# Second attention rebuilt with tokens on partitions, its projections and output products placed inside the attention steps, and gating products opened early

## The reference

```python
g = gelu(y); val, gate = split(g @ w_glu); x = x + val * sigmoid(gate)      # gating
...
kv = rms_norm(x, kv_norm) @ kv_w                 # keys and values from x
k = rms_norm(kv[..., :1024] as (8 heads, 2, 64), k_norm); v = kv[..., 1024:] as (8 heads, 128)
q = rms_norm((rms_norm(x, attn_norm) @ w_q) as (8 heads, 2, 64), q_norm)
s = q . k * scale + relative_bias, causal        # two score maps c = 0, 1 per head
pm = softmax(s)
attn = pm[c=0] - lam * pm[c=1]                   # lam from four learned vectors
o = attn @ v                                     # 128 wide per head
o = rms_norm(o, subln) * (1 - lam_init)          # over the 128 of a head
x = x + o @ w_o
```

## Time and profile before

| | |
|---|---|
| median of 3 runs | 2135.4 us (2134.31 to 2138.55) |
| profiled execution | 2137.13 us, its span 2135.3 us |
| TensorE busy | 2039.7 us, 96% of the span |
| VectorE, ScalarE, GpSimd busy | 1230.0, 816.9, 465.5 us |
| mean granted clock of TensorE | 0.974 |
| weight loads | 308 of 512 KB |

### The profile page before, as it was taken

One profiled execution on the slowest core, in us unless ns is written; L12 is line 12 of the kernel. 1 busy time (PEld: TensorE's weight loads), 2 busy tenths in 40 slices (PEclk: granted clock), 3 DMA queues, 4 the chain that ended last, 5 costly groups with the idle time before them and its releaser, 6 DMA issues.

```text
span 2135.3 us, 26693 instructions
## 1 busy us (share of the span) xinstructions
PE 2039.7 (96%) x9714; PEld 1621.7 (76%) x9714; DVE 1230.0 (58%) x1695; ACT 816.9 (38%) x1248; POOL 465.5 (22%) x626
## 2 busy tenths in 40 slices
PE   8999999999999879999999989999888999999988
PEld 7998678888887767877878877655564877877877
DVE  5345365656355984577365557533485577365555
ACT  4323242222135874344243335322364444243333
POOL 3110039998814551000000011011100100000010
PEclk9999799999999999999999999999897999999999
DMA  4221023264442422222223232211100222223232
GB/s 144 90 80 61 20 89 109 89 217 150 167 160 81 156 84 89 89 89 92 95 98 109 75 103 99 82 62 62 50 26 20 79 89 98 90 98 109 79 99 99
DMA packets 54866, 201.69 MB, mean 94 GB/s; under 512 B 6438, under 2 KB 6950, under 8 KB 53740
## 3 DMA queue, kind: packets, MB, share of 16 engines
q1 hardware_dynamic: 47132, 166.39, 23.1%
q0 software_dynamic: 7632, 33.91, 4.4%
HBM read 184.51 MB, written 15.77 MB: 94 GB/s over the span
## 4 chain that ended last, share of the span: by engine, by line
PE 86%; DVE 9%; ACT 2%; issue 1%; DMA 1%; POOLq 0%; POOL 0%; SPq 0%; DVEq 0%; ACTq 0%
PE ps L440 69%; PE ps L612 6%; PE ps L763 2%; PE ps L572 1%; PE ps L838 1%; PE ps L554 1%; DVE t L1793 1%; PE ps L1769 1%; DVE w_lo L426 1%; DVE t L1429 1%; DVE rstd L535 0%; DVE t L564 0%; PE ps L794 0%; PE ps L1760 0%; DVE pp L1609 0%
## 5 line engine op out<-in xcount | busy, mean ns | idle before, releaser
L440 PE MATMUL ps<-x_hi,w_hi 128*128 128x512 f32 x1280 | 512.4, 400 | 2.7 <-DVE w_lo L426 2.6
L440 PE MATMUL ps<-x_lo,w_hi 128*128 128x512 f32 x1280 | 507.8, 397 | 0.0
L440 PE MATMUL ps<-x_hi,w_lo 128*128 128x512 f32 x1280 | 505.4, 395 | 0.0
L426 DVE TENSOR_TENSOR w_lo<-raw,w_hi 128x1024 fp32r<-128x1024 f32 x308 | 401.6, 1307 | 173.0 <-ACT w_hi L422 172.7
L422 ACT ACTIVATE w_hi<-raw 128x1024 fp32r<-128x1024 f32 x308 | 321.7, 1048 | 216.3 <-DMA raw<-in_wstream 143.6
L440 PE MATMUL ps<-a_hi,w_hi 128*128 128x512 f32 x864 | 345.1, 399 | 10.7 <-DVE pp L1609 4.8
L440 PE MATMUL ps<-a_lo,w_hi 128*128 128x512 f32 x864 | 342.5, 396 | 0.0
L440 PE MATMUL ps<-a_hi,w_lo 128*128 128x512 f32 x864 | 342.5, 396 | 0.0
L440 PEld LDWEIGHTS ps<-x_hi,w_hi 128*128 128x128 f32 x1280 | 241.5, 189 | 83.9 <-issue 22.9
L440 PEld LDWEIGHTS ps<-x_hi,w_lo 128*128 128x128 f32 x1280 | 241.7, 189 | 55.7
L440 PEld LDWEIGHTS ps<-x_lo,w_hi 128*128 128x128 f32 x1280 | 241.4, 189 | 55.1 <-issue 1.2
(11 more groups left out here) (364 smaller groups left out, 2544.6 us busy)
## 6 DMA issues: line engine op xcount, KB each, us to landing
raw<-in_wstream SPq DMA_DIRECT2D x308, 512.0 KB, 3.3
ev<-mix_ev POOLq DMA_DIRECT2D x8, 1024.0 KB, 5.1
mix_cp<-c_p POOLq DMA_DIRECT2D x8, 640.0 KB, 3.5
cp<-mix_cp POOLq DMA_DIRECT2D x8, 640.0 KB, 6.3
mix_ev<-v_b POOLq DMA_DIRECT2D x8, 512.0 KB, 3.5
fall<-fall POOLq DMA_DIRECT2D x4, 544.0 KB, 5.1
h<-in_xT SPq DMA_DIRECT2D x4, 528.0 KB, 7.2
mix_ev<-e_r POOLq DMA_DIRECT2D x1, 2048.0 KB, 8.5
```

The source lines that it names most:

```text
L426: e.tensor_tensor(w_lo[:, u.slot, :], raw[:, u.c % 2, :], w_hi[:, u.slot, :], ALU.subtract)\
L440: last = e.matmul(ps[:, bank, :], wt[:, u.slot, w], x[:, k0 + k, 0:SEQ], start=(k == 0 and n == 0), stop=(k == kt - 1 and n == 2))
```

## The change

The projections of the second attention are made with the tokens on partitions. The activations become the stationary side (`a_hi`, `x_hi` blocks of 128 tokens) and the weights the moving one. Six groups of 96 matmuls (`group_pe`) take the place of 24 units: query heads 0 to 3 and 4 to 7, key 0 to 3, value 0 to 3, key 4 to 7, value 4 to 7. A group has eight parts of 12 matmuls: four weight blocks c for token blocks 0 and 1, then the same four for token blocks 2 and 3. The loads follow (`load_columns`): four unit tiles by 256 columns, later two by 512. ScalarE evicts with the token's norm as scale and squares (`group_act`), VectorE sums by head and scales (`head_sums_dve`, `head_scales_dve`). Query, key and output tiles of a head are turned by TensorE (`turn_pe`) into one bank (7) and split on the way out (`turn_act`, `turn_dve`); `TURN` numbers the turns in TensorE's order, and each waits for the one before (`tr_ev`).

The first four groups run ahead of the loop (`attention2_first`), the last two and the output products of the first four heads stand inside the steps (`FILL`: step to part). A head's blocks now run from the widest to the narrowest. The scores use a ring of three banks. The weights are left without the first map's divisor, which goes into the norm: the output is made as queries by features, held (`dve_hold`), squared with its sum (`act_square`) and scaled (`dve_out`, with a root on ScalarE, `act_root`), per query and head, then turned back by the flip matrix. The output products have 12 matmuls in each part (`out2_pe`); those of heads 4 to 7 follow the loop. Both barriers, `normed`, all `head_*` helpers, the values' turn, the subtractions on GpSimd and the load of `spread2` are gone. GpSimd's load of p now waits for the last value product. The sums for the token norm run as four products with one column.

Apart from this, four gating units are opened before and behind the last mixer's output products, with six of their eight tiles; two weight splits move ahead for it.

The core of the diff (mere renamings, tiles in memory and the semaphores' list are left out):

```diff
+    def glu_open_pe(e, s):
+        u = Unit(U_GLU + s)
+        e.wait_ge(lo_ok, u.n(1))
+        e.wait_ge(unit_ev, U_GLU)
+        if s >= 2:
+            e.wait_ge(v_ev, KT)
+        for k in range(GLU_K):
+            if s == 0:
+                e.wait_ge(g_lo, k + 1)
+            product(e, u, s, a_hi, a_lo, k, KT)
+    def glu_close_pe(e, s):
+        u = Unit(U_GLU + s)
+        for k in range(GLU_K, KT):
+            if s == 0:
+                e.wait_ge(g_lo, k + 1)
+            last = product(e, u, s, a_hi, a_lo, k, KT)
+        last.then_inc(unit_mm, 1)
...
+    NORMED = {0: 0, 1: 1, 2: 2, 4: 3}
+    FILL = {}
+    for k, i in enumerate((0, 1, 2, 3, 5, 6, 7, 8)):
+        FILL[i] = ("group", 4, k)
+    for k, i in enumerate((9, 10, 12, 13, 14, 16, 17, 18)):
+        FILL[i] = ("group", 5, k)
+    for k, i in enumerate((21, 22, 23, 25, 26, 28, 30, 32)):
+        FILL[i] = ("out", k // 2, k % 2)
+    SPLIT_AT = {}
+    for i, (kind, a, b) in FILL.items():
+        if kind == "group" and b >= 4:
+            SPLIT_AT[i + 1] = U_Q + 4 * a + b
+        elif kind == "out" and b == 1:
+            SPLIT_AT[i + 1] = U_WO + 4 + a
...
+    def load_columns(e, n, first, count, lo):
+        e.wait_ge(lo_ok, n - 1)
+        w = KT * P // count
+        src = A["wstream"][first * P:(first + count) * P, lo:lo + w].rearrange("(a p) c -> p a c", p=P)
+        e.dma_start(raw[:, n % 2, :].rearrange("p (a c) -> p a c", a=count), src).then_inc(raw_in[n % 2], 16)
+    def load_tail(e):
+        for g, first in enumerate((U_Q, U_Q + 4, U_KV, U_KV + 8, U_KV + 4, U_KV + 12)):
+            for c in range(4):
+                load_columns(e, U_Q + 4 * g + c, first, 4, 256 * c)
+        for j in range(KT):
+            load_columns(e, U_WO + j, U_WO + 2 * (j % 4), 2, SEQ * (j // 4))
...
+    def group_bank(g, tb):
+        return (0 if g < 4 and tb >= 2 else 3) + tb % 2
...
+    def group_pe(e, g, half):
+        s, c = half // 4, half % 4
+        n = U_Q + 4 * g + c
+        hi, lo = (a_hi, a_lo) if g < 2 else (x_hi, x_lo)
+        if s == 0:
+            e.wait_ge(lo_ok, n + 1)
+        if c == 0:
+            if g == 0:
+                e.wait_ge(unit_ev, U_Q - 2 + 2 * s)
+            elif g == 4 and s == 1:
+                e.wait_ge(unit_ev, U_Q + 18)
+            elif g == 5:
+                e.wait_ge(unit_ev, U_Q + 20 + 2 * s)
+            else:
+                e.wait_ge(unit_ev, U_Q + 4 * g - 2 + 2 * s)
+        for k in (2 * c, 2 * c + 1):
+            if s == 0 and g in (0, 2):
+                e.wait_ge(xlo_ok, (40 if g == 0 else 48) + k + 1)
+            for tb in (2 * s, 2 * s + 1):
+                o = ps[:, group_bank(g, tb), :].rearrange("p (a c) -> p a c", a=4)
+                r = slice(tb * P, (tb + 1) * P)
+                for i, (x, w) in enumerate(((hi, w_hi), (lo, w_hi), (hi, w_lo))):
+                    last = e.matmul(o, x[:, k, r], w[:, n % 4, :].rearrange("p (a k c) -> p k a c", a=4, k=2)[:, k % 2],
+                                    start=(k == 0 and i == 0), stop=(k == KT - 1 and i == 2))
+        if s == 1:
+            last.then_inc(unit_mm, 1)
+        elif c == 3:
+            last.then_inc(pg_mm, 1)
...
+    def group_act(e, g, tb):
+        if tb < 2:
+            e.wait_ge(pg_mm, g + 1)
+        else:
+            e.wait_ge(unit_mm, U_Q + 4 * g + 4)
+        if g == 0 and tb == 0:
+            e.wait_ge(rstd_ok, STEP[6] + 1)
+        src, r = ps[:, group_bank(g, tb), :], rstd[:, tb:tb + 1]
+        ins = e.activation(group_store(g, tb), src, ACT.Copy, scale=r)
+        if g in NORMED:
+            k = 4 * NORMED[g] + tb
+            ins.then_inc(qn_c, 1)
+            ge(e, qn_s, k - 1)
+            ins = e.activation(sq[:, k % 2, 0:SEQ], src, ACT.Square, scale=r)
+        ins.then_inc(unit_ev, 1)
...
+    def head_sums_dve(e, g, tb):
+        k = 4 * NORMED[g] + tb
+        e.wait_ge(unit_ev, U_Q + 4 * g + tb + 1)
+        e.reduce_sum(state[:, 3 * NORMED[g], 8 * tb:8 * tb + 8],
+                     sq[:, k % 2, 0:SEQ].rearrange("p (g c) -> p g c", c=HD), AX_X).then_inc(qn_s, 1)
+    def head_roots_act(e, g):
+        r = 3 * NORMED[g]
+        e.wait_ge(qn_s, 4 * NORMED[g] + 4)
+        e.activation(state[:, r + 1, :], state[:, r, :], ACT.Sqrt, bias=eps6[:, 0:1], scale=1.0 / HD).then_inc(qn_rt, 1)
+    def head_scales_dve(e, g):
+        r = 3 * NORMED[g]
+        e.wait_ge(qn_rt, NORMED[g] + 1)
+        n = dve.did(e.reciprocal(state[:, r + 2, :], state[:, r + 1, :]))
+        e.wait_ge(dve_did, n)
+        for tb in range(4):
+            y = group_store(g, tb).rearrange("p (g c) -> p g c", c=HD)
+            e.tensor_tensor(y, y, state[:, r + 2, 8 * tb:8 * tb + 8].unsqueeze(2).to_broadcast([P, 8, HD]), ALU.mult)\
+                .then_inc(qn_y, 1)
...
+    def turn_pe(e, kind, p):
+        k = TURN[kind, p]
+        if k == 0:
+            e.wait_ge(tab_ok, 2)
+        ge(e, tr_ev, k)
+        if kind == "o":
+            e.wait_ge(oy_ok, p + 1)
+            for qt in range(4):
+                last = e.matmul(ps[:, 7, qt * P:(qt + 1) * P], o_held(p)[:, qt, :], flip[:, :], start=True, stop=True)
+        else:
+            g = (p // 4) if kind == "q" else (2, 4)[p // 4]
+            e.wait_ge(qn_y, 4 * NORMED[g] + 4)
+            for tb in range(4):
+                last = e.transpose(ps[:, 7, tb * P:(tb + 1) * P], group_store(g, tb)[:, (p % 4) * P:(p % 4 + 1) * P],
+                                   ident[:, :])
+        last.then_inc(tr_mm, 1)
...
+    def out2_pe(e, j, h, ks):
+        n = U_WO + j
+        hi, lo = (o0_hi, o0_lo) if j < 4 else (o1_hi, o1_lo)
+        if ks[0] == 0:
+            e.wait_ge(lo_ok, n + 1)
+            if j == 5:
+                e.wait_ge(nb_ok, 64)
+            elif j == 6:
+                e.wait_ge(pt_ok, 32)
+                e.wait_ge(od_ok, 32)
+            elif j == 7 and h == 0:
+                e.wait_ge(tr_ev, len(TURNS))
+            elif h == 0:
+                if j:
+                    e.wait_ge(wo_ev, j)
                 else:
+                    e.wait_ge(unit_ev, U_WO)
+            else:
+                e.wait_ge(unit_ev, U_WO + (4 if j == 7 else j) + (j == 7))
+        for k in ks:
+            e.wait_ge(tr_ev, TURN["o", 4 * (j // 4) + k] + 1)
+            w = slice(SEQ * h + k * P, SEQ * h + (k + 1) * P)
+            for i, (wt, x) in enumerate(((w_hi, hi), (w_hi, lo), (w_lo, hi))):
+                last = e.matmul(ps[:, out2_bank(j, h), :], wt[:, n % 4, w], x[:, k, :], start=(k == 0 and i == 0),
+                                stop=(k == 3 and i == 2))
+        if ks[-1] == 3:
+            last.then_inc(unit_mm if h else wo_mm, 1)
...
-            if g >= 2:
-                e.wait_ge(nb_ok, 2 * (g - 1))
-            for n, (a, b) in enumerate(((q_hi, k_hi), (q_hi, k_lo), (q_lo, k_hi))):
+            p, qt, N = step(g)
+            if g % 4 == 0:
+                e.wait_ge(tr_ev, TURN["k", p] + 1)
+            if g == 0:
+                e.wait_ge(unit_ev, U_Q + 16)
+            ge(e, nb_ok, 2 * g - 1)
+            for n, (a, b) in enumerate(((qr_hi, kr_hi), (qr_hi, kr_lo), (qr_lo, kr_hi))):
                 for c in range(2):
                     r = slice(HD * c, HD * c + HD)
-                    last = e.matmul(ps[:, 2 * sl + c, 0:N], a[r, p, qt * P:(qt + 1) * P], b[r, p, 0:N],
+                    last = e.matmul(ps[:, (2 * g + c) % 3, 0:N], a[r, p % 2, qt * P:(qt + 1) * P], b[r, p % 2, 0:N],
...
-                last = e.matmul(ps[:, 4 + sl, j * P:(j + 1) * P], ST[g % 3][:, 0, j * P:(j + 1) * P], flip[:, :],
-                                start=True, stop=True)
+                last = e.transpose(ps[:, 5, j * P:(j + 1) * P], ST[g % 3][:, 0, j * P:(j + 1) * P], ident[:, :])
...
-                last = e.matmul(ps[:, 6 + p % 2, qt * P:(qt + 1) * P], vtok[:, p % 2, j, :], pt2[:, sl, j, :],
+                last = e.matmul(ps[:, 6, 0:P], PT2[g % 2][:, j * P:(j + 1) * P], v_tok[:, j, p * P:(p + 1) * P],
...
-            n = dve.did(e.reciprocal(small[:, 3, k:k + 2], small[:, 2, k:k + 2]))
+            n = dve.did(e.reciprocal(small[:, 3, k:k + 1], small[:, 2, k:k + 1]))
             e.wait_ge(dve_did, n)
-            n = dve.did(e.tensor_tensor(small[:, 3, k:k + 2], lam_pair[:, :], small[:, 3, k:k + 2], ALU.mult))
-            e.wait_ge(dve_did, n)
-            n = dve.did(e.tensor_scalar(t[:, 0, 0:N], t[:, 0, 0:N], small[:, 3, k:k + 1], None, ALU.mult))
+            n = dve.did(e.scalar_tensor_tensor(small[:, 3, k + 1:k + 2], col(15, g), lam_pair[:, 1:2], small[:, 3, k:k + 1],
+                                               ALU.mult, ALU.mult))
...
+        def dve_hold(g):
+            p, qt, N = step(g)
+            e.wait_ge(pv_mm, g + 1)
+            if g % 4 == 0 and p >= 2:
+                e.wait_ge(tr_mm, TURN["o", p - 2] + 1)
+            e.tensor_copy(o_held(p)[:, qt, :], ps[:, 6, 0:P]).then_inc(od_ok, 1)
         def dve_out(p):
+            r = slice(4 * p, 4 * p + 4)
+            e.wait_ge(os_ok, 4 * p + 4)
```

(99 more changed lines are left out.)

501 lines of the change are left out of this document (234 added, 267 removed).

## The result

The changed kernel takes 2106.6 us (median of 4 runs, 2104.71 to 2107.65) where the kernel before took 2136.6 in the same runs (2134.31 to 2138.55): a ratio of 0.986 (95% interval 0.984 to 0.988), 30 us less. Forecast were 2077 and a range of 2046 to 2104. The direction was right; the gain is half of the 58 us of the forecast, and the time lies 2.6 us above the range. The profiled execution took 2104.7 us (span 2102.9).

A forecast was written before the change was run, and what follows sets the result against it. TensorE's work was taken to bound the projections, a mixture of three engines the loop. 98.2 before the loop, 176 in it and 23.9 after make 298 against 352 us: 54 less, 58 with gating, so 2077, range 2046 to 2104.

The forecast's parts named there:

- Behind a split: 2.4: Before the loop: the first scores wait 2.4 us for the last group's banks, which ScalarE empties behind a split.
- The loop's work: In the loop: TensorE's own work 126 us, 59 for the heads and 67.4 for filled-in parts, plus 9 for gaps.
- The loop's waits: In the loop: output norm 17 us, first steps 5, banks and keys' norm 14, splits 5, less 5 for sheltering.
- Output turns: In a head's last step: TensorE's turn waits for the output norm's chain on other engines, 17 us in all.
- banks: In steps 5, 9 and 14: groups 4 and 5 reuse two banks and wait for ScalarE's evictions, 11 us.
- The prediction's last sign of being wrong: In the loop: parts waiting for evictions longer than 5 us, making the loop longer than any rival would.
- The 2.2 us lost in rows 2 followed some 4 us of waiting; 5 for all: In the loop: TensorE's lowered clock after waits costs 5 us, judged from one profiled loss behind a wait.
- Rival 2: In the loop: waits keep the clock at 1.2 GHz; half of it gives 2105 us, all 2128; chance 0.13.
- Rival 1: In the loop: parts shelter the waits, TensorE bounds it at 140 to 150 us, total 2041 to 2051; chance 0.19.
- Rival 3: In the loop: 16 table switches each hold ScalarE 1.4 us more than the load, 2088 to 2099 us; chance 0.03.
- Rival 4: Weight loads by columns: above 8.8 us a load TensorE waits, the gain gone at 12.4; chance 0.05.
- Gating: Around the last mixer's output products: gating units opened early fill TensorE's idle time, gain 4 us, from 0 to 6.

The follow-up runs named there:

- run 3: The changed kernel with the fourth weight split of each early group put behind the evictions, roots and lambda exponential: 2102.8 us, ratio 0.9839.
- run 8: The changed kernel with three changes of order together (late split behind evictions, evictions in their own step, output turn one step later): 2089.0 us, ratio 0.9768.
- run 17: The kernel of run 11 with the table loads put back by an unread root, in no chain of the norm: 2080.1 us, ratio 0.9724.
- run 11: The kernel of run 8 with a copy in place of the root of the output's norm, which is left out: 2066.4 us, ratio 0.9679.
- Run 4: The changed kernel with ScalarE evicting groups 4 and 5 in the step of their last part instead of the next: 2100.5 us, ratio 0.9835.
- Run 9: The changed kernel with eight idle products on TensorE ahead of the wait of five output turns: 2107.4 us, ratio 0.9871.
- Run 13: The kernel of run 8 with the output norm's root on GpSimd, VectorE's product with the factor ahead of the next step's maxima: 2089.9 us, ratio 0.9777.
- run 1: The kernel before with only the early opening of four gating units and the two weight splits moved for it: 2132.7 us, ratio 0.9986.
- run 7: The changed kernel with the sums of squares ahead of the last FFN on VectorE instead of GpSimd: 2104.9 us, ratio 0.9842.
- runs 11 to 15: The kernel of run 8 with the output norm's root copied or on GpSimd, product placed differently, once without Newton steps: 2066.4, 2089.1, 2089.9, 2086.2, 2075.6 us.

## Why the prediction was wrong in size

**Ahead of the loop the clock has no term.** From the second query unit on, the first group took 20.1 us (forecast 17.9), since its first 24 products ran at the low clock; lambda's gap 8.3 (7.3); three groups and the first turns 73.5 (70.6), 288 products in place of which 67.5 us were counted at the full clock; the wait of the first scores 2.65 (2.4). The 6.9 us lost by the clock are as much as the 6.4 us of excess. "Behind a split: 2.4" came out by luck: ScalarE's list has four splits there, the last behind a load, and TensorE's slower products covered most of it. In run 3, which mends this order, that wait is 1.2 us shorter and the kernel 4 us faster.

**The loop's work** was right. Loop less waits is 151.1 us in the changed kernel, 148.1 in run 8, 144.6 in run 17 and 142.3 in run 11, while the waits of 0.4 us and more go from 39.8 over 28.0 and 21.1 to 15.7. From the first to the last, 24.1 us of waits less bring 8.8 of slow work less, 0.37 for each. Carried on to no waits, this leaves 136.5 us, an estimate: forecast were 126 and 9 for gaps. The granted clock says the same directly. Busy time times the missing share of the clock, in pieces of 0.5 us, is 15.6, 11.8, 8.2 and 6.2 us in these four traces, and busy time less that is 134.5 to 134.9 us in each.

**The loop's waits** were right in sum, 36 us after the 5 that shelter each other (17 + 5 + 14 + 5 - 5) against 39.8, and less so in detail. Output turns came to 12.9 (17), banks to 10.3 (11), first steps without a part to 5.2 (5), the keys' norm to 2.6 (3). No group part in the loop waited for a split (5). 2.3 us at the loop's end had no term. One more was missed: the value product of step 19 waits 5.0 us for the last value group, whose last part stands in step 18 and which ScalarE evicts in 19. The forecast named only the parts that reuse a bank. Run 4 removed it. The prediction's last sign of being wrong, a part that waits for an eviction for over 5 us, came true in one place (5.58 us at 1492.35).

**The clock is the step that failed.** "The 2.2 us lost in rows 2 followed some 4 us of waiting; 5 for all" is the mis-sized term: 151.1 less 136.5 is some 14.5 us in the loop (15.6 by the granted clock), where 5 stood, and 6.9 us ahead of it, where nothing stood. The prediction read 0.55 us lost for each us of waiting from its row; with 36 us of forecast waits that is 20, and a loop of 191. It held a ratio in hand and did not multiply it. That 191 meets the 190.9 measured is partly luck: TensorE's idle time at that row is 3.07 us, not 4, which would make the ratio 0.7, and the loop's own is 0.37. Rival 2 priced the clock only for one that is low half of the time. Its 2105 lies near the 2106.6, by luck as well: the low clock held for some 42 of the loop's 190.9 us. Run 9 sets a bound to this reading: where the clock was raised behind five waits, three quarters of what the work gained turned into new waits. So the 14.5 us are the difference in the sum, not what a remedy for the clock alone would give back. A sum of TensorE's work and its waits treats both as independent, and in this loop they aren't.

**Rivals.** Rival 1 (parts shelter the waits) is refuted by the 39.8 us. Rival 3 needed 1.4 us more for each switch: the rows show 1283 ns and the next operation at once. The rule of the Trainium skill that went with it (ScalarE: Activation LUTs, Table sets: the hidden batching unit), exponentials together and roots together, is borne out by run 11 against run 17, 10 to 14 us for 13 loads. Run 13 against run 8 can't tell, since its chain is longer. Rival 4 is refuted: the 28 loads from 1340 to 1640 took 3.4 us in the median, and no group part in the loop waits for `w_lo`.

**Gating and the rest.** Forecast were 4; by the traces the FFN behind it starts 4.6 us earlier (906.21 to 910.85), by run 1 it is 3. Behind the loop it is 24.3 (23.9). The FFN's opening had no term and costs 2.3. 1.4 us of it are TensorE's waits for low halves of VectorE (1.26) and for GpSimd's sums (0.17); run 7 took the sums from GpSimd and left the stretch as long, so its cause stays open. Of the 4.6 us of the gating 3.1 are left at the second query unit (1340.33 to 1337.23); a projection between lost 1.5 at the low clock. The sum of the parts: 58 forecast, less 6.4, 15, 0.4, 2.3 and 1.5, is 32. The two profiled executions differ by 32.4, the medians by 30.

## What to carry to other kernels

Where three engines pass work around in fixed order, add up the waits and then multiply them by what the trace shows the clock to lose behind a wait, ahead of the loop as well: here some 0.4 us for each. An operation that needs nothing late (an eviction) should not stand in a list behind one that does (a split behind a load). And one experiment that removes two things at once, a table load and the length of the chain it stands in, shows the price of neither: put each back by itself before the cause is named, and measure in the traces what is called the same in two runs.

## What the runs showed of the hardware

- Thirteen table loads of 1283 ns, 16.7 us of ScalarE's time, cost 10 to 14 us in the loop though no chain of the norm ran through them (runs 17 and 11). A us more of chain from sums to product cost about a us in each head (runs 11 to 15).
- Idle products into a bank that is overwritten anyway raise TensorE's clock within a wait (the turn behind one took 1.16 us instead of 2.05), at no cost here and no gain either (run 9).
- A wait does not lower the clock every time: in the changed kernel's loop it was low behind 10 of 15 waits, among them one of 1.92 us, and not behind one of 3.08.
- Loads of 512 KB in runs of 1 and 2 KB took 3.4 us in the median from 1340 to 1640 (3.7 for the 13 inside the loop), hardly more than the 3.3 in runs of 4 KB, and products with the weights as the moving side, read in runs of 128, kept their pace (57.5 us for 240 in the chain). No row of before had shown either.
- GpSimd's operations of 128x4 took 0.18 to 0.20 us in a chain and followed each other at 0.28, less than the 0.25 to 0.52 of most of 128x32.
